# The down projections of two feed-forward layers: two passes over full rows, or seven passes of quarter products

## What is computed

```python
def swiglu(u, wg, wu, wd):
    return (jax.nn.silu(u @ wg) * (u @ wu)) @ wd          # hidden width D_FF = 2816

x = layer_norm(ALPHA * x + 0.5 * (1.0 + g1) * swiglu(u, ffn1_wg[l], ffn1_wu[l], ffn1_wd[l]), ln_g[l, 0], ln_b[l, 0])
...   # attention and output projection between the two
x = layer_norm(ALPHA * x + 0.5 * (1.0 + g3) * swiglu(u, ffn2_wg[l], ffn2_wu[l], ffn2_wd[l]), ln_g[l, 2], ln_b[l, 2])
```

## Time and profile before

| | us |
|---|---|
| median of 3 runs | 2314.64 (2311.70 to 2315.34) |
| the profiled execution | 2314.72 |
| its span | 2312.7 |
| down phase of ffn1, from its first matmul (471.8) to its last gate product (713.0) | 241.2 |
| down phase of ffn2, the same stretch (2058.9 to 2300.1) | 241.2 |

### The profile page before, as it was taken

One profiled execution on the slowest core, in us unless ns is written; L12 is line 12 of the kernel. 1 busy time (PEld: TensorE's weight loads), 2 busy tenths in 40 slices (PEclk: granted clock), 3 DMA queues, 4 the chain that ended last, 5 costly groups with the idle time before them and its releaser, 6 DMA issues. The chain is left out here.

```text
span 2312.7 us, 29070 instructions
## 1 busy us (share of the span) xinstructions
PE 2185.2 (94%) x10641; PEld 1826.7 (79%) x10641; DVE 1395.9 (60%) x2194; ACT 954.7 (41%) x1866; POOL 529.8 (23%) x538
## 2 busy tenths in 40 slices
...
GB/s 258 108 169 168 166 164 164 155 252 144 141 119 18 140 49 27 117 1 1 1 1 1 1 1 1 1 141 32 115 96 82 82 83 82 83 198 232 147 166 85
DMA packets 171314, 230.83 MB, mean 100 GB/s; under 512 B 15713, under 2 KB 114081, under 8 KB 171176
## 3 DMA queue, kind: packets, MB, share of 16 engines
...
## 5 line engine op out<-in xcount | busy, mean ns | idle before, releaser
L722 DVE TENSOR_TENSOR ffn2A_u<-ffn2A_u,ffn_banks 128x512 f32<-128x512 f32 x60 | 41.2, 687 | 126.3 <-PE ffn_banks L669 120.0
L2391 ACT ACTIVATE nsaa_exps<-nsaa_scores,nsaa_neg_max 128x64 f32<-128x64 f32 (+8 forms) x192 | 108.0, 577 | 16.1 <-DVE nsaa_neg_max L2422 15.6
L1060 DVE SCALAR_TENSOR_TENSOR late_part_late<-ada_rows,far_silu_c,late_part_late 128x1024 f32<-128x1024 f32 x56 | 106.4, 1900 | 5.1 <-DMA ada_rows<-in_w_ada 5.0
L2422 DVE TENSOR_REDUCE nsaa_neg_max<-nsaa_scores 128x1 f32<-128x640 f32 (+8 forms) x104 | 90.3, 871 | 28.8 <-PE nsaa_scores L2347 28.2
L2437 DVE TENSOR_TENSOR nsaa_turned_lo<-nsaa_ring,nsaa_turned_hi 128x512 fp32r<-128x512 f32 (+1 forms) x148 | 97.6, 685 | 15.3 <-ACT nsaa_turned_hi L2400 13.8
L1744 PE MATMUL in_acc<-in_w_hi,mix_in_u_hi 128*128 128x494 f32 x256 | 99.4, 388 | 7.3 <-DVE in_w_lo L1707 7.3
L546 ACT ACTIVATE ffn1A_t_hi<-ffn1A_t 128x512 fp32r<-128x512 f32 x80 | 48.5, 628 | 133.9 <-POOL ffn1A_t L539 102.5
L546 ACT ACTIVATE ffn2A_t_hi<-ffn2A_t 128x512 fp32r<-128x512 f32 x80 | 48.4, 628 | 124.3 <-POOL ffn2A_t L539 93.6
L1744 PE MATMUL in_acc<-in_w_lo,mix_in_u_hi 128*128 128x494 f32 x256 | 99.1, 387 | 0.0
L1744 PE MATMUL in_acc<-in_w_hi,mix_in_u_lo 128*128 128x494 f32 x256 | 99.0, 387 | 0.0
L2400 ACT ACTIVATE nsaa_turned_hi<-nsaa_ring 128x512 fp32r<-128x512 f32 (+1 forms) x148 | 84.1, 600 | 26.9 <-PE nsaa_ring L2359 24.5
...
## 6 DMA issues: line engine op xcount, KB each, us to landing
ada_rows<-in_w_ada POOLq DMA_DIRECT2D x56, 512.0 KB, 4.6
ffn_raw_g<-in_ffn_wg SPq DMA_DIRECT2D x44, 512.0 KB, 3.7
ffn_raw_u<-in_ffn_wu SPq DMA_DIRECT2D x44, 512.0 KB, 4.9
ffn_raw_g<-in_ffn_wd SPq DMA_DIRECT2D x44, 512.0 KB, 3.6
...
ffn_raw_u<-in_ffn_wd SPq DMA_DIRECT2D x44, 512.0 KB, 3.7
early_w<-in_w_ada SPq DMA_DIRECT2D x16, 512.0 KB, 7.1
...
```

What stands on the lines that cost most here:

```text
L722: dve.tensor_tensor(out, base, bank, ALU.add).then_inc(self.mixed, 1)
L1060: dve.scalar_tensor_tensor(out=part_late[:, v, :], in0=ada[:, n % 2, :], scalar=silu_c[:, k:k + 1], in1=part_late[:, v, :], op0=ALU.mult, ...
L2391: made = act.activation(exps[n % slots][:, r, 0:u.widths[r]], scores[:, m % 2, u.columns(r)], ACT.Exp, bias=neg_max[:, n % SUMS, r:r + 1], ...
L2422: top = dve.reduce_max(at, rows, AX, negate=True)
```

## The change

The down phase becomes 77 steps in seven passes of 11 (`PAIRS` = FC // 2 pairs of chunks). The hidden matrix is seen as four quarters: chunk parity (even or odd chunks) by row half; the weights as chunk parity by column half. A pass makes one product of a sum of hidden quarters and a sum of weight quarters, over 11 pairs of chunks; a step is one pair: operands of 128x512 (hidden) and 128x512 (weight), stored side by side as one 128x1024 tile, and 4 output blocks with three matmuls each, 12 in all. Passes use two groups of four banks (`QUAD`) in the order P1, P5, P6, P2, P3, P7, P4. P6, P7 and P4 add onto what their group holds.

- Sums of hidden quarters are made by DMA: GpSimd issues 44 accumulating DMAs a layer (`add_hidden`, DRAM onto SBUF, 256 KB each), at most four in flight. Sums of weight quarters are made by DVE (`blend_weight`, 128x512, 44 a layer). They live in an 11-tile buffer `pair`, which three later passes reuse.
- There are seven raw slots in place of two (`SLOTS`), so SP runs up to seven steps ahead of DVE. Their loads are 256 KB each.
- ACT copies the results of P1 and P5 out of PSUM (`keep`). DVE joins results (`take`), multiplies by the gate and adds to x (`settle`); `down` places these.
- Scaling of x: in ffn1 on ACT; in ffn2 one DVE operation and one accumulating DMA of the scaled offset row, SBUF onto SBUF, a tile.
- Two operations of the up phase (`mix` with n = 2 and `plain_hidden` with t = 1) become SCALAR_TENSOR_TENSOR of the same size, for a sign.
- End of ffn2: the offset row is first broadcast into 768 rows of the output in DRAM (3 MB, DRAM to DRAM). The first four tiles then need no addition on GpSimd, which stores them accumulating; tiles 4 and 5 (`SHARED` = 6) are normalised by ACT, multiplied by the gain on GpSimd and stored the same way; tiles 6 and 7 stay on DVE. Statistics of one column half of tiles 4 to 7 are taken before the last pass ends.

```diff
-STEPS = 2 * FC
-GROW = 7
-LAST_AT = (4, 7, 10, 13)
-RING = 5
-DRAIN = FC + 3
+PAIRS = FC // 2
+P1, P5, P6, P2, P3, P7, P4 = range(7)
+QUAD = (0, 1, 0, 1, 1, 0, 0)
+JOINS = (False, False, True, False, False, True, True)
+STEPS = 7 * PAIRS
+RING, SLOTS, LANES = 5, 7, 4
+COPY_AT, BACK_AT, GROW_AT, PAIR_AT, LAST_PAIR_AT = 3, 22, 22, 8, 50
+LAST_AT = (61, 64, 67, 70)
+SHARED = 6
...
+    def fill(self, sp, n):
+        p, j = divmod(n, PAIRS)
...
+        elif n >= SLOTS:
+            self.slot_vacant(sp, n - SLOTS)
+        h, w, done = self.slot(n)[:, 0:HALF], self.slot(n)[:, HALF:D], self.slot_in[n % SLOTS]
+        if p in (P1, P2, P7):
...
+            sp.dma_start(h, self.hidden_at(f, 0)).then_inc(done, 16)
+        f, e = {P1: (0, 0), P5: (0, 0), P6: (1, 1), P2: (1, 0), P3: (1, 1), P7: (1, 1)}[p]
+        sp.dma_start(w, self.weight_at(2 * j + f, e)).then_inc(done, 16)
+        if p == P7:
...
+            sp.dma_start(self.b12[:, j % LANES, :], self.weight_at(2 * j, 1)).then_inc(self.b12_in[j % LANES], 16)
...
+    def add_hidden(self, pool, p, j):
...
+        pool.dma_start(place, self.hidden_at(2 * j + f, t), accum_op=ALU.add).then_inc(done, 16)
...
     def step(self, pe, n):
...
+        p, j = divmod(n, PAIRS)
+        pe.wait_ge(self.d_split, cut_no(n))
+        for i in range(4):
+            if j == 0:
+                self.bank_ready(pe, p, i)
+            last = self.multiply(pe, n, i)
...
+    def take(self, dve, p, i):
...
+        dve.wait_ge(self.y_done, 4 * p + i + 1)
...
+        elif p == P7:
+            dve.wait_ge(self.taken, TAKEN[P6] + i + 1)
+            dve.tensor_tensor(p5, bank, p5, ALU.subtract).then_inc(self.taken, 1)
...
+    def settle(self, dve, p, i):
...
+            dve.tensor_tensor(y, y, self.gate[:, cols], ALU.mult).then_inc(self.gated, 1)
+            dve.wait_ge(self.gated, WEIGHED[p] + i + 1)
+        dve.tensor_tensor(x, x, y, ALU.add).then_inc(self.drained, 1)
+    def down(self, dve, n):
+        if n:
+            if (n + 2) // PAIRS in (P5, P6, P7):
+                self.blend_weight(dve, n + 2)
+            self.split_step(dve, n)
+        if n // PAIRS == P2:
+            self.blend_weight(dve, n)
+        for p in (P6, P2, P3, P7):
+            first = (p + 1) * PAIRS + COPY_AT
+            if n == first:
+                for i in range(4):
+                    self.take(dve, p, i)
+            if p != P6 and first < n <= first + 4:
+                self.settle(dve, p, n - first - 1)
...
@@ SP, end of ffn1's up phase (ffn2 alike)
         for n in range(3):
-            ffn.load_step(sp, n)
+            ffn.fill(sp, n)
         ffn.store_hidden(sp, FC - 1)
-        ffn.load_step(sp, 3)
         sp.wait_ge(ffn.made, made_all(FC - 1))
...
+        for n in range(3, P4 * PAIRS):
+            ffn.fill(sp, n)
...
+            if PAIR_AT <= n < PAIR_AT + PAIRS:
+                ffn.fill_pair(sp, n - PAIR_AT)
...
@@ GpSimd, ffn2
+        for p in (P5, P6, P3):
+            for j in range(PAIRS):
+                ffn.add_hidden(pool, p, j)
+        pool.wait_ge(offset_grown, 1)
+        for i in range(TT):
+            pool.wait_ge(grown_half, i + 1)
+            pool.dma_start(x_sb[:, i, :], ffn.offset_rows[:, :], accum_op=ALU.add).then_inc(ffn.grown, 16)
+        for j in range(PAIRS):
+            ffn.add_hidden(pool, P7, j)
+        pool.wait_ge(based, 16)
...
+            pool.dma_start(out_dram[0, i * P:(i + 1) * P, :], x_sb[:, i, :], accum_op=ALU.add).then_inc(stored_first, 16)
+        for i in range(TT // 2, SHARED):
+            pool.wait_ge(final.normed, i + 1)
+            pool.tensor_tensor(x_sb[:, i, :], x_sb[:, i, :], g_row[:, :], ALU.mult).then_inc(pool_scaled, 1)
+            pool.wait_ge(pool_scaled, i - TT // 2 + 1)
+            pool.dma_start(out_dram[0, i * P:(i + 1) * P, :], x_sb[:, i, :], accum_op=ALU.add).then_inc(stored_first, 16)
```

More of the change, by code:

```diff
@@ new lines, in operand, with operand_ready @@
+    def operand(self, n, part):
+        p, j = divmod(n, PAIRS)
+        if p in (P5, P6, P4) or (p == P3 and part.start == 0):
+            return self.pair[:, j, part]
+        return self.slot(n)[:, part]
+    def operand_ready(self, act, n):
+        p, j = divmod(n, PAIRS)
+        if p in (P1, P2, P3):
+            self.slot_landed(act, n)
+        if p in (P5, P6, P3, P7):
+            self.hidden_added(act, p, j)
+        if p in (P5, P6, P7):
+            act.wait_ge(self.t_done, t_no(n))
+        if p == P4:
+            act.wait_ge(self.last_in[j % LANES], 16 * (j // LANES + 1))
+            act.wait_ge(self.t_done, t_no(P2 * PAIRS + j))
@@ L811, in step @@
[L811 to L830 removed]
+        for part in parts_of(n):
+            act.activation(self.d_hi[n % RING][:, part], self.operand(n, part), ACT.Copy).then_inc(self.d_rounded, 1)
@@ new lines, in multiply @@
+    def multiply(self, pe, n, i):
+        p, j = divmod(n, PAIRS)
+        hi, lo = self.d_hi[n % RING], self.d_lo[n % RING]
+        rows = slice(i * P, (i + 1) * P)
+        for at, (h, w) in enumerate(((hi, hi), (hi, lo), (lo, hi))):
+            last = pe.matmul(self.banks[:, 4 * QUAD[p] + i, :], h[:, rows], w[:, HALF:D], start=(j == 0 and at == 0 and not JOINS[p]),
+                             stop=(j == PAIRS - 1 and at == 2), skip_group_check=True)
+        return last
+    def step(self, pe, n):
+        p, j = divmod(n, PAIRS)
+        pe.wait_ge(self.d_split, cut_no(n))
[3 more added lines that the diff above has]
+            last = self.multiply(pe, n, i)
+            if j == PAIRS - 1:
```

441 lines of the change are left out of this document (264 added, 177 removed).

## The result

The changed kernel takes 2321.64 us (median of 9 runs, 2316.68 to 2323.3), the kernel before 2315.26 beside it (9 runs). The ratio is 1.0024, 95% interval 1.0015 to 1.0033: slower by some 6 us, where 2260 and a gain of 54 us were forecast. The profiled execution has a span of 2318.6 us, against 2312.7.

The account below looks back on a forecast made before the run. PE's matmuls were taken to bound the down phases. ffn1 -28.9, ffn2 -27.6 and +2 for DMA sum to -54.5 us, from 2314.7 to 2260; forecast 2254 to 2264 (chance 0.60), range 2252 to 2282.

Parts of the forecast that it names:

- DMA term: Unevenness of DMA in ffn2, an accumulating DMA priced near a plain copy: +2 us.
- rival 1: DMA binds the down phases if accumulations cost the engines their bytes twice: 5 to 25 us above forecast, 2265 to 2285; chance 0.20.
- ffn1, first to last start: ffn1's down phase: 132 fewer matmuls at 0.2267 us give -29.9, with +1.7 at its start and -0.2 between passes.
- step 3 late: Start of each down phase: step 3's load waits for the last hidden chunk's store; +1.7 us in ffn1, +2.4 in ffn2.
- stall at P4: PE enters P4 in banks DVE has just to take: 0.5 us in ffn1, 1.3 in ffn2 (0.7 to 2.7).
- stall at P3: PE enters P3 in banks DVE has just to take: 0.7 us in ffn1, 0.5 in ffn2.
- between the phases: Behind ffn1's last gate product one DVE addition of 0.69 less: -0.5 us.
- end behind ffn2's last start: Work behind ffn2's last matmul: less for DVE, part given back beside GpSimd; -0.5 us, bounds -2.1 to +3.6.
- rival 4: The saving isn't there because PE's matmuls of smaller groups start less densely; no chance of its own given.
- Rival 2: DVE binds in ffn2, with stalls at P4 and the last steps and a dear tail: +3 to +8 us, 2263 to 2268; chance 0.10.
- Rival 3: Slower than before: POOL's accumulating queue paces PE, from 4.0 us a unit in ffn2, 5.5 in ffn1; chance 0.05.
- The tail: Behind ffn2's last matmul: up to 4.8 us given back to GpSimd contention, 0.8 taken; -0.5 us, dear bound +3.6.

Follow-up runs that it names:

- plain copies and early broadcast: Changed kernel with all 96 accumulating DMAs as plain copies (sums left out, not the reference) and the broadcast in six pieces in ffn2's up phase: 2258.7 us.
- plain copies alone: Changed kernel with its 88 hidden-half and 8 offset-row accumulating DMAs as plain copies, sums left out, broadcast unmoved: 2268.5 us.
- all edits: Changed kernel with broadcast early, offsets and hidden sums (P5, P6, P3 in ffn1; P5, P3 in ffn2) on DVE, ffn2's x scaled every third step: 2271.5 us.
- the tail on DVE: Changed kernel with broadcast early and offset rows added by DVE, plus SHARED = 4 so DVE normalises tiles 4 and 5: 2288.6 us.

## Why the prediction was wrong

**The DMA term failed.** The prediction put **+2** for all DMA effects, "near the copies". With the kernel of plain copies and early broadcast as the measure, it is 2321.6 - 2258.7 = **62.9**: 53.1 for the adding, 9.8 for the broadcast's place. The sign of the result came from this term; all others together were off by some 3 us, partly because they cancel (below). No row of before showed an accumulating DMA, and the nearest rows were plain copies of the same queue. Where the thing that differs is the very thing that costs, the nearest row gives no price. The text took the cheap end for its term.

The dear end was there as rival 1, at 0.20, with twice the bytes and 5 to 25 us. Its price was right: twice, as measured. The Trainium skill (Collectives: The Full Stack, "The bandwidth ceiling: the fold count and why AG ≠ RS ≠ AR") says of ring collectives that the adding step runs at half the rate of the copying one, since it reads two sources; the 188 against 370 GB/s agree. HBM was read for 225.30 MB with and without the adding: the second source lies in SBUF here, so the profile's bytes don't show it. What was wrong was the effect of the price, three times over:

- *It was averaged over the phase.* Twice the bytes gave ffn1 180 us of 213, "hidden, but for P5 and P7". But P5 asks for three loads and an accumulation a step: 3 x 0.262 MB at 370 GB/s and one at 188 are 2.1 + 1.4 = 3.5 us, against 2.72 of matmuls. In ffn1 the engines were full from 480 to 580 (1.06 to 1.09), and did nothing from 660 to 680 (0.00). The seven slots covered it in part only: 9.5 us of ffn1 went (223.2 against 213.7), before any broadcast or offset.
- *What comes together wasn't put together.* The offsets (4.2 MB, 22 us at 188 GB/s), the two rows, the broadcast and P2's loads all meet at 2142 to 2170. The prediction spread them over 213 us.
- *The order of SP's queue.* The prediction asked how POOL's queue paces PE, not how SP's does: the broadcast stood ahead of every later load. The weight load issued at 2165.38 let ACT start only at 2193.15, 27.8 us after. In the kernel before that broadcast didn't exist. Its bytes, 3.1 MB, are 8 us at 400 GB/s; moving it to a quieter place gave 16.4. With plain copies around it, it gave 9.8, little more than the bytes. Whether the rest is its place in SP's queue, as this text argues, or its meeting the accumulations on the same engines, no run separates: none issues it at the same moment from another queue.

The capacity of the engines was not over- but underestimated: 360 GB/s was inferred from the earlier trace rows, 413 is there. It wouldn't have saved the sum, since adding takes the time, not the bytes. And the sign that the prediction named, a DMA share under 0.9 in every pass, was too strict: with plain copies the share was 1.04 and PE did not wait.

**The other terms**, read in the kernel with plain copies and the broadcast early, where DMA is out of the way:

| term | forecast | measured |
|---|---|---|
| ffn1, first to last start | 240.8 - 29.9 + 1.7 - 0.2 = 212.4 | 214.2 |
| ffn2, first to last start | 240.8 - 29.9 + 2.4 + 0.4 = 213.7 | 211.9 |
| step 3 late, ffn1 and ffn2 | +1.7, +2.4 | 2.0, 1.2 |
| stall at P4, ffn1 and ffn2 | 0.5, 1.3 | 0.5, 0.5 |
| stall at P3, ffn1 and ffn2 | 0.7, 0.5 | none, none |
| between the phases, from ffn1's last start to ffn2's first | 1346.4 - 0.5 = 1345.9 | 1342.4 |
| end behind ffn2's last start | 13.0 - 0.5 = 12.5 (10.9 to 16.6) | 14.8 |

These misses are +1.8, -1.8, -3.5 and +2.3, and nothing shows of the +2 for DMA. Together they leave the span of this kernel's profile (2255.2) 3.0 us under the forecast one (2258.2). That it comes so near is in part luck: the largest of them lies between the down phases, which the change hardly touches. That stretch was 1348.5 us in the changed kernel and 1347.3 with plain copies alone; no run tells why.

ffn1's missing 1.8 us stand for the most part in the window of its start: PE lost the 2.0 at step 3 from 480 on and then had a granted clock of 0.50 between 484 and 486 (0.91 over the window), so that 72 matmuls took 18.0 us, not 16.3. A stall costs more than its length where the clock falls behind it, and no term counted that:

```profile
480.00:500.00 20.00, 18.02 (x72) 14.57 (x72) 10.60 (x10) 9.99 (x10) 2.19 (x4) 0.91 1.05 395
```

The matmuls kept their pitch (90 in 20 us, as before), so rival 4 is out. In the changed kernel P4's stall in ffn2 was 2.2, inside 0.7 to 2.7. Rival 2 (DVE binds in ffn2) didn't come true either: with plain copies and the broadcast early DVE has the changed kernel's work, and PE waited 1.7 us in all of ffn2. DVE became the bound only in the kernel with all edits, which gives it 22 sums of 0.69 and 8 additions of 1.22 more in ffn2, 25 us. Rival 3 had the sign right and the mechanism wrong: it asked for 4.0 us a unit of 256 KB before the kernel is slower; by its engine time a unit takes 1.4 (188 GB/s), and its landing after 8.3 us stayed under the 10.9 allowed. The kernel was slower all the same, because the accumulations take the engines from the loads, whose landing came to 12.6 us from 9.5 with plain copies.

**The tail** came out between its forecast and the dear bound. Of the changed kernel, behind the last matmul:

```profile
2304.40 1.22 DVE L294 SCALAR_TENSOR_TENSOR ffn_last_minus_mean<-ffn_last_mv,ffn_last_rstd 128x1 f32<-128x1 f32 x1
...
2306.93 3.47 DVE L1692 SCALAR_TENSOR_TENSOR mix_out_x<-mix_out_x,ffn_last_rstd,ffn_b_row 128x1024 f32<-128x1024 f32 x1
2306.98 2.33 POOL L1499 TENSOR_TENSOR mix_out_x<-mix_out_x,ffn_g_row 128x1024 f32<-128x1024 f32 x1 [0.21 <-ACT mix_out_x L312]
```

The first multiplication of GpSimd runs from 2303.21 on; DVE's 128x1 operation beside it took 1.22 where it took 0.16 just before. The 128x1024 operation took 3.47 beside the second one, where its like took 1.28 in the kernel with the tail on DVE. Together 3.3 us are given back, of the 4.8 that the prediction allowed and the 0.8 that it took; with the 1.3 forecast as the gain without contention this makes +2.0, against +1.3 (14.4 us in the changed kernel, 13.0 before) and +1.8 (14.8) measured. The rule of the Trainium skill (SBUF — State Buffer, "Who interferes with whom") that such a pair contends for a port agrees with these rows; the 3.3 measured lie nearer to the 4.8 that it allows than to the 0.8 that was chosen.

The chance of "slower" was 0.05, and all of it lay in rival 3. It should have stood on rival 1's mechanism, a DMA bound whose size was open.
